# Attention's output stores moved from SyncE's queue to ScalarE's, in a one-core decoder step

## The chip, the cores and the metric

One Trainium2 chip, one core of it. The kernel is one launch. Its time is device microseconds of that core; the time before is the median of three runs, 2228.45 us (2225.63 to 2229.6). One more execution was profiled, and the rows below are from it.

Engines: PE is TensorE, DVE VectorE, ACT ScalarE, POOL GpSimd, SP SyncE. SP computes nothing here; it issues DMAs. A DMA that an engine issues stands in that engine's instruction stream: what it waits for, everything behind it on that engine waits for too.

## The reference

One step of a two-layer decoder trunk, float32, for a prompt of 1024 tokens and 8 samples of one token each: a pooling mixer and a gated ConvFFN, then keys and values (shared) and queries, dilated attention, and a second ConvFFN. The change lies in the prompt's attention. It has three groups of 8 heads of 64, with dilations 1, 4 and 16, in blocks of 128 queries that see their own block and the one before:

```
s = einsum('bnqrhe,bnkrhe->bnrhqk', qb, kk)
s = where(mask, s, NEG_INF)
lse = logsumexp(s, axis=-1)
p = exp(s - lse)
o = einsum('bnrhqk,bnkrhe->bnqrhe', p, vv)
...
wts = softmax(stack(lses))          # over the three groups
o = sum(wts * stack(outs))
```

## The kernel before

The work runs in stages, one behind the other on every engine: pooling, ConvFFN 0, projection of k, v and q (into DRAM, `kvs` and `qs`), attention, merge (the weighted sum of the groups, and the output projection w_o), ConvFFN 1. In attention, some 205 us long, every engine has one unrolled loop over half-steps.

**Steps.** `STEPS` (L2080) has 24 steps of 128 queries: 8 for dilation 1, 8 for dilation 4, 8 for dilation 16. Step s has two half-steps, i = 2s and 2s + 1, of four heads each (`NH` is 48). A step is wide if it also sees the block before: steps 1 to 7 and the odd ones of 9 to 15. The rest are narrow.

**One half-step i.** PE (`pe_attention`, L2234) makes the scores of i, turns (transposes) the queries or keys of the next step, turns the probabilities of i - 1 (`turn_p`) and multiplies those of i - 2 with v (`outputs`, L2297). DVE (`dve_attention`) takes the negated maxima of i (`maxima`, L2362) into `osb`, copies the turned queries or keys (L2354), copies the turned probabilities of i - 1 (L2366), and copies the outputs of i - 2 into `osb` (L2372, L2373; the second counts `at_oc`); in between it reduces one product of the samples' scores (L2390). ACT (`act_attention`, L2460) makes four exponentials of i (L2470), each with a row sum into `osb`, counted by `at_e`, and, for a wide i - 1, copies half of its turned probabilities (L2476). POOL multiplies the samples' cached keys (`kc`) with their queries (`qb`).

**osb and its stores.** `osb` has three slots, one a step (s % 3): outputs, maxima and sums, 528 floats for each of 128 queries. `store_o(e, s)` (L2222) waits for `at_oc` and `at_e` at 2s + 2 and issues the slot's store into `os_` in DRAM: one DMA of 264 KB for dilations 1 and 4, two of 132 KB for dilation 16. `maxima` of step s waits, from step 3 on, for the store of step s - 3 to have landed (L2360):

```
if s >= 3:
    v.wait_ge(rows_out[s % 3], ROWS + moved(s - 3, 3))
```

**SP's loop** (`sp_attention`, L2139) has 27 passes. Pass s issues, in this order: the queries of step s + 1 (`load_q`, waits for PE to have turned those of s - 1), k and v of step s (`load_kv`, into a ring `kvt` of four; waits for PE's outputs of step s - 3 if that is wide, else of s - 4), the store of step s - 3, two sample loads (`load_sample`; a buffer of `kc` waits for POOL's product), one of five copies to the outputs, cached values of one sample in passes 11 to 14 and 17 to 20 (`load_v`, L2210), and in pass 24 three quarters of w_o (`load_wo`, L2501). After it `sp_merge` (L2504) waits for all stores and loads `om` out of `os_`. ACT's merge begins with the splits of w_o (L2654).

Of the kernel before, what the change touches and what calls it, by code (L numbers as in the profile page):

```python
# [59 lines left out]
def build(nc, a, o):  # L60

    with ExitStack() as ctx:
# [2020 lines left out]
        NSTEP, NH = len(STEPS), 2 * len(STEPS)  # L2083

        def tile_rows(src, s):

            g, n, r, _ = STEPS[s]
            if g == 0:
                return [(slice(0, P), src[n * P:(n + 1) * P, :])]
            if g == 1:  # L2090
                return [(slice(0, P), src.rearrange("(m r) c -> r m c", r=4)[r, n * P:(n + 1) * P, :])]
            v = src.rearrange("(u r) c -> r u c", r=16)
            return [(slice(64 * e, 64 * e + 64), v[2 * n + e]) for e in range(2)]
# [9 lines left out]
        def wide(i):  # L2103

            return STEPS[i // 2][3]

        def span(i):

            return 2 * P if wide(i) else P
# [29 lines left out]
        def sp_attention(sp):  # L2139

            sp.wait_ge(pj_pe, 27 * GROUPS)

            def load_q(s):
                if s >= 2:
                    sp.wait_ge(at_tp, 2 * s - 3)
                for part, src in tile_rows(qs[STEPS[s][0], 0:T], s):
                    sp.dma_start(qt[part, s % 2, :], src).then_inc(at_q[s % 2], 16)

            def load_kv(s):
                if s >= 4:  # L2150
                    sp.wait_ge(at_o, 2 * s - 4 if STEPS[s - 3][3] else 2 * s - 6)
                for part, src in tile_rows(kvs[STEPS[s][0], 0:T].rearrange("t c n -> t (c n)"), s):
                    sp.dma_start(kvt[part, s % 4, :], src).then_inc(at_kv[s % 4], 16)

            def load_sample(n):
                s, g = n // 3, n % 3
                if g == 0:
                    if s >= 2:
                        sp.wait_ge(sm_p, n - 3)
                    sp.dma_start(qb[:, s % 2, :, :], qs[:, T + s, :].partition_broadcast(P)).then_inc(sm_q[s % 2], 16)  # L2160
                if n >= 3:
                    sp.wait_ge(sm_p, n - 2)
                sp.dma_start(kc[0:KEYS[g], n % 3, :], a[CACHES[g]][s, ::DIL[g], 0].rearrange(
                    "t h e -> t (h e)")).then_inc(sm_k[n % 3], 16)

            load_q(1)
            load_kv(1)
            sp.wait_ge(pj_h, 12 * GROUPS)
            sp.wait_ge(pj_l, 12 * GROUPS)
            for i in range(3):  # L2170
                sp.wait_ge(rows_out[i], ROWS)
            for g in range(GROUPS):
                sp.dma_start(qn[:, g, :], qs[g, T:N, :]).then_inc(in_new, 16)
                sp.dma_start(stage[0:NS, g, :], kvs[g, T:N].rearrange("t c n -> t (c n)")).then_inc(in_new, 16)
            sp.dma_start(samp[:, :], a["samp"]).then_inc(in_new, 16)
            for s in range(NSTEP + 3):
                if 1 <= s < NSTEP:
                    if s + 1 < NSTEP:
                        load_q(s + 1)
                    if s > 1:  # L2180
                        load_kv(s)
                if s >= 3:
                    store_o(sp, s - 3)
                for n in (2 * s - 4, 2 * s - 3):
                    if 0 <= n < ST:
                        load_sample(n)
                if 4 <= s < 4 + len(KV_PARTS):

                    g, first, rows, name = KV_PARTS[s - 4]
                    dst = (o[name + "_prompt"][0] if first < T else o[name + "_sample"][:, 0]).rearrange("t c h e -> t c (h e)")  # L2190
                    at = first - (T - WIN[g]) if first < T else 0
                    sp.dma_start(dst[at:at + rows], kvs[g, first:first + rows]).then_inc(out_w, 16)
                if s == 17:
                    sp.wait_ge(sm_p, ST)
                    sp.dma_start(diag, a["diag"]).then_inc(in_diag, 16)
                for n in {11: [4], 12: [5], 13: [6], 14: [7], 17: [0], 18: [1], 19: [2], 20: [3]}.get(s, []):
                    load_v(sp, n)
                if s == NSTEP:
                    sp.wait_ge(sm_st, 12)
                    for k in range(3):  # L2200
                        load_wo(sp, k)
# [8 lines left out]
        def load_v(e, s):  # L2210
            if s == 3:
                e.wait_ge(sm_o, 3)
            for g in range(GROUPS):
                e.dma_start(values_of(s, g)[0:KEYS[g], :], a[CACHES[g]][s, ::DIL[g], 1].rearrange(
                    "t h e -> t (h e)")).then_inc(sm_vin[s % 3], 16)
# [6 lines left out]
        def store_o(e, s):  # L2222
            e.wait_ge(at_oc, 2 * s + 2)
            e.wait_ge(at_e, 2 * s + 2)
            for part, dst in tile_rows(os_[STEPS[s][0]], s):
                e.dma_start(dst, osb[part, s % 3, :]).then_inc(rows_out[s % 3], 16)

        def scores_out(i):


            b = 2 * (i % 2)
            return ps[:, b:b + 2, 0:2 * span(i)].rearrange("p b (h n) -> p b h n", h=2)
# [227 lines left out]
        def act_attention(act):  # L2460
            for i in range(NH + 2):
                if i < NH:
                    s, n = i // 2, span(i)
                    act.wait_ge(at_m, i + 1)
                    if i >= 2:
                        act.wait_ge(at_pt, i - 1)
                    src = scores_out(i)
                    for j in range(4):
                        h = 4 * (i % 2) + j
                        ins = nc.scalar.activation(prob[:, i % 2, j * n:(j + 1) * n], src[:, j % 2, j // 2, :], ACT.Exp,  # L2470
                                                   bias=osb[:, s % 3, QW + h:QW + h + 1],
                                                   accum_out=osb[:, s % 3, QW + HEADS + h:QW + HEADS + h + 1])
                    ins.then_inc(at_e, 1)
                if 0 < i <= NH and wide(i - 1):
                    act.wait_ge(at_pt, i)
                    nc.scalar.activation(probT[:, (i - 1) % 2, 512:1024], ps[:, 5, :], ACT.Copy).then_inc(at_pb, 1)  # L2476
                if i == H_SM:
                    act.wait_ge(sm_st, 1)
                    nc.scalar.activation(sall, ps[0:64, 5, 0:SK], ACT.Exp, bias=stat[:, 0:1],
                                         accum_out=stat[:, 1:2]).then_inc(sm_e, 1)  # L2480

        def pool_attention(q):
            q.wait_ge(pj_r, 5 * 18 * GROUPS)
            q.wait_ge(pj_s, 1 + 7 * 18 * GROUPS)
            nc.gpsimd.memset(pT, 0.0).then_inc(sm_z, 1)
            for n in range(ST):
                s, g = n // 3, n % 3
                if g == 0:
                    q.wait_ge(sm_q[s % 2], 16 * (s // 2 + 1))
                q.wait_ge(sm_k[n % 3], 16 * (n // 3 + 1))  # L2490
                wait(q, sm_r, n)
                nc.gpsimd.tensor_tensor(prod[0:KEYS[g], 0, :], kc[0:KEYS[g], n % 3, :], qb[0:KEYS[g], s % 2, g, :],
                                        ALU.mult).then_inc(sm_p, 1)
# [7 lines left out]
        def load_wo(e, k):  # L2501
            e.dma_start(stage[:, k % 3, :], a["w_o"][0, k * P:(k + 1) * P, :]).then_inc(piece_in[k % 3], 16)
# [251 lines left out]
        @block.sync  # L2754
        def _(sp):
            sp_start(sp)

            def begin0(e, n):
                if n == 1:
                    sp_pool_tails(e)  # L2760
                    e.wait_ge(wp_l, 1)
                    e.wait_ge(wp_h, 1)
            sp_ffn(sp, 0, ffn[0], begin0, pool_x)
            sp_project(sp)
            sp_attention(sp)
            sp_merge(sp)

            def begin1(e, n):
                e.wait_ge(wo_h, 4)
                e.wait_ge(wo_l, 4)  # L2770
            sp_ffn(sp, 1, ffn[1], begin1, wo_x)

            sp.wait_ge(out_w, 16 * (3 + len(KV_PARTS)))
            sp.wait_ge(tl_out, 32)
            sp.wait_ge(ct_out[0], 32 * 6 * DEPTH)
            sp.wait_ge(ct_out[1], 32 * 5 * DEPTH)
            sp.wait_ge(y_out, 16 * STORES)
# [132 lines left out]
```

## Time and profile before

| | |
|---|---|
| median of three runs | 2228.45 us |
| the profiled execution | 2229.66 us |
| its span in the trace | 2227.8 us |
| attention in it | about 1225 to 1430 us |
| busy: PE, DVE, ACT, POOL | 97%, 69%, 44%, 22% |
| mean DMA rate | 172 GB/s |
| queue q1 (issued by SP) | 284.24 MB, 39.5% of 16 engines |
| queue q10 (issued by ACT) | 4.68 MB, 0.6% |

The 1.9 us between span and time lie around the program. All times of rows are microseconds from the start of the span, unless ns is written. A group of instructions has its line in the kernel, its engine, its operation, output<-input by the program's names, and xcount. Brackets at the end of a timeline's row tell how long the engine was idle before it, and what released it. DMA-issuing instructions (SPq, ACTq) take part in the engine's order but are not counted as busy; the time to landing is from the issue until the data is there.

### The profile page before, as it was taken

The page shows a single profiled execution, that of the slowest core. Times are in us where ns is not written, and L with a number is a line of the kernel's source. Part 1 is how long each engine was busy: PE and PEld are TensorE (multiplying, and loading weights), DVE is VectorE, ACT ScalarE, POOL GpSimd, SP SyncE. Part 2 cuts the span into 40 slices and gives each one's busy share as a digit, 9 for nine tenths or more (in the row PEclk, how much of TensorE's full clock was granted, in tenths as well). Part 3 has the DMA queues.
Part 4 walks back from the last instruction along what each step waited for, and adds up shares of the span by engine and source line. Part 5 has one row for each costly group of instructions (what it writes and reads, how often), then busy time and mean ns, then how long its engine had stood idle before and what let it go on. Part 6 is the DMA issues. An engine that isn't in the chain of part 4 may idle for free.

```text
span 2227.8 us, 43164 instructions
## 1 busy us (share of the span) xinstructions
PE 2171.4 (97%) x16008; PEld 2022.9 (91%) x16019; DVE 1536.4 (69%) x2375; ACT 988.5 (44%) x1868; POOL 480.2 (22%) x674
## 2 busy tenths in 40 slices
PE   7999999999999999999999999999999999999998
PEld 7999999999999977777777887598999999999998
DVE  4778888887656677365463777676888888875554
ACT  4655555555434533122121444455555555554342
POOL 1002223222200145053251220010122233221000
PEclk8999999999999999999999999999999999999999
DMA  6225777788985522222232797631467777889764
GB/s 188 86 83 162 200 207 189 190 216 214 295 258 180 171 94 81 100 81 95 95 104 103 244 285 195 188 124 48 129 171 206 208 192 200 205 228 318 213 193 140
DMA packets 243995, 383.28 MB, mean 172 GB/s; under 512 B 21736, under 2 KB 117784, under 8 KB 241971
## 3 DMA queue, kind: packets, MB, share of 16 engines
q1 hardware_dynamic: 207778, 284.24, 39.5%
q0 software_dynamic: 31328, 92.66, 19.1%
q10 hardware_dynamic: 4760, 4.68, 0.6%
q8 instruction: 80, 1.31, 0.2%
q14 instruction: 49, 0.39, 0.1%
HBM read 303.65 MB, written 173.98 MB: 214 GB/s over the span
## 4 chain that ended last, share of the span: by engine, by line
PE 91%; DVE 4%; DMA 3%; ACT 2%; issue 1%; SPq 0%; ACTq 0%; POOL 0%; DVEq 0%; POOLq 0%
PE ps L1233 38%; PE ps L1323 20%; PE ps L2065 6%; PE ps L2067 6%; PE ps L2066 6%; PE ps L2297 2%; PE ps L2710 2%; PE ps L2270 1%; DMA kvt<-kvs 1%; PE ps L2281 1%; PE ps L418 1%; PE ps L2237 1%; PE ps L853 1%; PE ps L2059 1%; PE ps L2060 1%; PE ps L479 1%
## 5 line engine op out<-in xcount | busy, mean ns | idle before, releaser
L1233 PE MATMUL ps<-hT,w 128*128 128x258 f32 x2752 | 462.1, 285 | 4.2 <-DVE w L1075 2.3
L1233 PEld LDWEIGHTS ps<-hT,w 128*128 128x128 f32 x2752 | 388.1, 191 | 5.1 <-DVE w L1075 2.7
L1233 PE MATMUL ps<-lT,w 128*128 128x258 f32 x1376 | 278.2, 284 | 0.0
L1233 PE MATMUL ps<-hB,w 128*128 128x258 f32 x1344 | 231.7, 284 | 3.7 <-DVE ub L1434 3.7
L2065 PE MATMUL ps<-wq,xh 128*128 128x512 f32 x576 | 227.7, 395 | 0.9 <-DVE wq L1892 0.9
L2067 PE MATMUL ps<-wq,xl 128*128 128x512 f32 x576 | 227.4, 395 | 0.0
L2066 PE MATMUL ps<-wq,xh 128*128 128x512 f32 x576 | 226.9, 394 | 0.0
L1233 PEld LDWEIGHTS ps<-lT,w 128*128 128x128 f32 x1376 | 215.2, 191 | 0.0
L1323 PE MATMUL ps<-gdh,wda 128*128 128x258 f32 x1184 | 198.9, 284 | 0.0
L1233 PEld LDWEIGHTS ps<-hB,w 128*128 128x128 f32 x1344 | 193.1, 192 | 4.1 <-DVE ub L1434 4.1
L1323 PE MATMUL ps<-gdh,wdb 128*128 128x258 f32 x1152 | 193.4, 284 | 0.0
L1323 PEld LDWEIGHTS ps<-gdh,wda 128*128 128x128 f32 x1184 | 166.7, 190 | 0.7 <-DVE gdl L1523 0.3
L1323 PEld LDWEIGHTS ps<-gdh,wdb 128*128 128x128 f32 x1152 | 161.7, 189 | 0.7
L1233 PE MATMUL ps<-lB,w 128*128 128x258 f32 x672 | 136.7, 285 | 0.0
L1184 ACT ACTIVATE w<-sq 128x1024 fp32r<-128x1024 f32 x84 | 89.0, 1059 | 107.6 <-PE ps L1233 91.9
L2065 PEld LDWEIGHTS ps<-wq,xh 128*128 128x128 f32 x576 | 108.2, 188 | 29.9 <-DVE wq L1892 4.3
L1459 DVE SCALAR_TENSOR_TENSOR ca<-ua,cwT,ca 128x1024 f32<-128x1024 f32 x88 | 112.8, 1281 | 28.8 <-ACT ca L1689 28.2
L1557 POOL DMA_DIRECT2D wsum<-in_w_down x44 | 24.1, 554 | 501.7 <-DMA stage<-in_w_up 423.4
L2067 PEld LDWEIGHTS ps<-wq,xl 128*128 128x128 f32 x576 | 108.0, 188 | 25.4
L2066 PEld LDWEIGHTS ps<-wq,xh 128*128 128x128 f32 x576 | 108.2, 188 | 25.1
L1560 POOL DMA_DIRECT2D wsum<-in_w_down x88 | 80.3, 1096 | 225.6 <-DMA stage<-in_w_up 176.0
L2470 ACT ACTIVATE prob<-ps,osb 128x128 f32<-128x128 f32 (+1 forms) x192 | 77.2, 414 | 106.3 <-DVE osb L2362 106.3
(338 smaller groups left out, 4839.2 us busy)
## 6 DMA issues: line engine op xcount, KB each, us to landing
stage<-in_w_up SPq DMA_DIRECT2D x176, 256.0 KB, 3.8
wsum<-in_w_down POOLq DMA_DIRECT2D x132, 256.0 KB, 5.4
gs<-cb SPq DMA_DIRECT2D x44, 516.0 KB, 6.7
stage<-wsum SPq DMA_DIRECT2D x88, 256.0 KB, 3.0
tsum<-gs POOLq DMA_DIRECT2D x66, 258.0 KB, 7.4
tsum<-gneg POOLq DMA_DIRECT2D x66, 258.0 KB, 7.9
stage<-in_w_down SPq DMA_DIRECT2D x58, 256.0 KB, 3.1
stage<-in_w_kv SPq DMA_DIRECT2D x24, 512.0 KB, 3.9
```

The lines of the kernel that those rows point to most:

```text
L1184: nc.scalar.activation(out, src, ACT.Copy).then_inc(f_hi, 1)
L1233: mm = pe.matmul(ps[:, bank + c, 0:HB], w, m[:, c * HB:(c + 1) * HB], start=(first and i == 0), stop=(i == len(parts) - 1), skip_group_che ...
L1323: mm = pe.matmul(ps[:, 2 * d + c, 0:HB], w, m[:, c * HB:(c + 1) * HB], start=(i in FRESH and p == 0 and j == 0), stop=(last and j == 2), s ...
L1459: nc.vector.scalar_tensor_tensor(out=c[:, 0:T], in0=u[:, t:t + T], scalar=w, in1=c[:, 0:T], op0=ALU.mult, op1=ALU.add).then_inc(f_conv, 1)
L1557: q.dma_start(dst, src).then_inc(sums_in, 16)
L1560: q.dma_start(dst, src, accum_op=ALU.add, max_dma_last_dim=4 * N).then_inc(sums_in, 16)
L2065: pe.matmul(out, xh[:, k, tok], W, start=(k == 0), stop=False)
L2066: pe.matmul(out, xh[:, k, tok], Wt, start=False, stop=False)
L2067: mm = pe.matmul(out, xl[:, k, tok], W, start=False, stop=(k == KC - 1))
L2297: mm = pe.matmul(ps[:, 6, j * P:(j + 1) * P], probT[:, i % 2, n * P:(n + 1) * P], v, start=(w == 0), stop=(w == len(tiles) - 1))
L2470: ins = nc.scalar.activation(prob[:, i % 2, j * n:(j + 1) * n], src[:, j % 2, j // 2, :], ACT.Exp, bias=osb[:, s % 3, QW + h:QW + h + 1], ...
L2710: mm = pe.matmul(ps[:, bank0 + n, 0:NW], w, m[:, c * NW:(c + 1) * NW], start=(i == 0), stop=(i == len(parts) - 1))
```

## The change

SP issues no store of `osb` any more. ACT issues that of step i / 2 - 2 in its half-step i, for even i from 4 on, behind the exponentials of i and the copy of i - 1, and the last one after its loop. Waits, sizes, order of the stores and semaphores are the same.

```diff
@@ sp_attention, SP's loop
                         load_q(s + 1)
                     if s > 1:
                         load_kv(s)
-                if s >= 3:
-                    store_o(sp, s - 3)
                 for n in (2 * s - 4, 2 * s - 3):
                     if 0 <= n < ST:
                         load_sample(n)
@@ act_attention, ACT's loop
                 if 0 < i <= NH and wide(i - 1):
                     act.wait_ge(at_pt, i)
                     nc.scalar.activation(probT[:, (i - 1) % 2, 512:1024], ps[:, 5, :], ACT.Copy).then_inc(at_pb, 1)
+                if i >= 4 and i % 2 == 0:
+                    store_o(act, i // 2 - 2)
                 if i == H_SM:
                     act.wait_ge(sm_st, 1)
                     nc.scalar.activation(sall, ps[0:64, 5, 0:SK], ACT.Exp, bias=stat[:, 0:1],
                                          accum_out=stat[:, 1:2]).then_inc(sm_e, 1)
+
+            store_o(act, NSTEP - 1)
```

## Rows read from the trace of the kernel before

**Rows 1.** The page: the chain that ended last, shares of the span by engine
```profile
PE 91%; DVE 4%; DMA 3%; ACT 2%; issue 1%; SPq 0%; ACTq 0%; POOL 0%; DVEq 0%; POOLq 0%
```

**Rows 2.** Stretches: length, busy time of each engine, PE clock, DMA share, GB/s
```profile
1297.00:1345.00 48.00, 43.81 (x417) 38.29 (x419) 36.52 (x70) 21.76 (x96) 15.07 (x12) 1.00 0.94 289
...
1405.00:1430.00 25.00, 23.54 (x212) 20.28 (x211) 19.75 (x45) 13.61 (x66) 0.00 (x0) 1.00 0.57 160
```

**Rows 3.** Waits of PE, 1225 to 1440: us in total, times, longest
```profile
PE ps L2237 <- DMA kvt<-kvs: 4.9, 5, 1.9
```

**Rows 4.** Timeline of PE: start, duration, instruction, idle before; keys of steps 12, 13
```profile
1328.26 0.66 PE L2237 MATMUL ps<-ident,kvt 128*128 128x128 f32 x4 [1.87 <-DMA kvt<-kvs]
...
1336.60 0.66 PE L2237 MATMUL ps<-ident,kvt 128*128 128x128 f32 x4 [0.94 <-DMA kvt<-kvs]
```

**Rows 5.** Waits of SP's queue, 1220 to 1500: us in total, times, longest
```profile
SPq L2226 <- DVE osb L2373: 45.4, 14, 5.0
```

**Rows 6.** Timeline of SP's issues, passes 11 to 13
```profile
1309.84 0.43 SPq L2153 DMA_DIRECT2D kvt<-kvs  x1
1314.19 0.33 SPq L2226 DMA_DIRECT2D os_<-osb  x1
...
1316.44 2.39 SPq L2214 DMA_DIRECT2D vlate<-in_cache_kv_w  x3
...
1321.45 0.33 SPq L2153 DMA_DIRECT2D kvt<-kvs  x1
...
1326.67 0.43 SPq L2153 DMA_DIRECT2D kvt<-kvs  x1
```

**Rows 7.** Tiles osb and y: stores issued, ns min/median/max; landing of osb's, us
```profile
L2226 SPq DMA_DIRECT2D os_<-osb x32: 326/448/1246, 1240.5 to 1430.5; - x32
...
DMA to landing us min/median/max: 2.0/4.0/7.0
...
L1798 ACTq DMA_DIRECT2D out_y_prompt<-yst x10: 379/483/1915, 2121.0 to 2224.1; - x10
```

**Rows 8.** Timelines of DVE and ACT around the maxima of step 12
```profile
1324.16 0.69 DVE L2390 TENSOR_REDUCE sq<-prod 128x8 f32<-128x512 f32 x1 [2.21 <-POOL prod L2492]
...
1327.38 0.48 ACT L2470 ACTIVATE prob<-ps,osb 128x256 f32<-128x256 f32 x1
...
1331.71 0.67 DVE L2362 TENSOR_REDUCE osb<-ps 128x4 f32<-128x512 f32 x1
```

**Rows 9.** Timelines, steps 20 and 21: ACT, SP, DVE, ACT, PE
```profile
1406.62 0.37 ACT L2470 ACTIVATE prob<-ps,osb 128x128 f32<-128x128 f32 x1
...
1410.06 1.11 SPq L2226 DMA_DIRECT2D os_<-osb  x2
...
1410.41 0.69 DVE L2362 TENSOR_REDUCE osb<-ps 128x4 f32<-128x512 f32 x1 [0.38 <-PE ps L2270]
...
1411.13 0.37 ACT L2470 ACTIVATE prob<-ps,osb 128x128 f32<-128x128 f32 x1 [1.16 <-DVE osb L2362]
...
1413.56 0.60 PE L2281 MATMUL ps<-ident,prob 128*128 128x128 f32 x4
```

**Rows 10.** DMA issues: KB each, median us to landing; 1300 to 1345, then 1405 to 1425
```profile
os_<-osb SPq DMA_DIRECT2D x5, 264.0 KB, 6.1
...
stage<-in_w_o SPq DMA_DIRECT2D x3, 512.0 KB, 6.5
...
os_<-osb SPq DMA_DIRECT2D x6, 132.0 KB, 2.3
```

**Rows 11.** Timelines of SP, ACT and DVE at attention's end
```profile
1411.21 1.24 SPq L2153 DMA_DIRECT2D kvt<-kvs  x2
...
1422.30 1.55 SPq L2502 DMA_DIRECT2D stage<-in_w_o  x3
...
1430.69 1.06 ACT L2654 ACTIVATE woh<-stage 128x1024 fp32r<-128x1024 f32 x1 [0.18 <-DMA stage<-in_w_o]
...
1437.20 0.18 DVE L2529 TENSOR_REDUCE ow<-om 128x8 f32<-128x24 f32 x1 [3.77 <-DMA om<-os_]
```

## The prediction

> **What bounds the kernel now.** I read the chain that ended last first [rows 1]: TensorE (PE) carries 91% of it, DMA 3%, ScalarE (ACT) 2%. A change on the queues of ACT and SP pays only where PE stands still for them. Then the stretches of attention [rows 2]: in the middle one, 1297 to 1345 us, PE is idle for 4.2 us of 48 and the DMA engines are 94% busy; in the last, 1405 to 1430, PE is idle for 1.5 us of 25 and the DMA engines are 57% busy. Next, whom PE waits for between 1225 and 1440 us [rows 3]: 4.9 us in five waits for loads of kvt, and any help for the loads must come out of them. The timeline of PE shows the waits singly; the two that matter here are 1.87 and 0.94 us [rows 4], for the k of steps 12 and 13.
>
> What do the stores do to SP? Its own waits [rows 5] name 45.4 us in 14 waits at L2226 for DVE's last copy of a step. That looks large, but most of what stands behind the wait could not start anyway. load_q(s+2), the next in line after the samples, needs the queries of step s turned, which PE does one half-step after the outputs that store_o(s-3) waits for. After a wide step load_kv(s), ahead of the store, waits for the same outputs (at_o 2s-4) itself. So the store holds back only the sample loads, the cache values (load_v) and the output copies, and those only where step s-3 is narrow and load_kv(s) needs two half-steps less.
>
> [Rows 6] show such a place: kvt of step 11 is issued at 1309.84, the store at 1314.19 as soon as DVE lets it, and load_v at 1316.44 behind the store and the samples; then kvt of step 12 at 1321.45, when PE has freed its buffer, and that of step 13 only at 1326.67, behind a store, three sample loads (one waits for POOL's product), three of load_v and the queries: 9 issues in 5.2 us, 4.5 at 0.5 each, and 0.7 of waiting.
>
> **Removed from SP.** 24 calls of store_o, 32 DMAs (16 of 264 KB, 16 of 132 KB), 32 x 0.448 = 14.3 us of issuing [rows 7], and the 45.4 us of waiting. What it is worth:
> - *Step 12's load.* The samples and load_v between 1314.5 and 1318.8 can go after 1310.3, so some 1.5 to 4 us earlier, bounded by POOL's products, for which kc's buffers wait. The load that PE misses is issued by PE's own outputs, so only its landing can improve, with 1.5 us less of backlog before it: 1.4 of the 1.87 us.
> - *Step 13's load.* One store issue (0.4) and the 0.7 of waiting go, if the samples come earlier, so it is issued about 1.1 us earlier; against a wait of 0.94 us, but PE also asks for it 1.4 us earlier by the first point. I take 0.4.
> - *The other three waits* (4.9 - 1.87 - 0.94 = 2.1) are for loads that PE's outputs release: nothing. Their bounds are 0 and all 2.1 us.
> - *DVE's 2.21 us wait for POOL's product* [rows 8] goes with the earlier samples; it lies beside PE's wait for kvt, so it is worth 0 by itself.
> Sum: -1.8 us, bounds 0 and -4.9 (all of the waits for kvt).
>
> **Added to ACT.** 32 issues. The nearest rows are the same store on SP, 0.33 to 1.25 us, median 0.45, and ACT's own stores of y, median 0.48 [rows 7]. The wait is no wait: store_o(i/2-2) wants at_oc and at_e at i-2; DVE makes the copies of half-step i-3 before maxima(i), and ACT has already waited for maxima(i). Issuing stands behind the exponentials of an even half-step, in ACT's idle time before the next: 1.16 us before those of 1411.13 in narrow steps [rows 9], for two DMAs that took SP 1.11 us, and more in wide ones. If it overran, PE would ask for these probabilities at 1413.56, when four exponentials of 0.37 us from 1411.13 are over at 1412.6: 0.95 us in reserve. Zero, cover named; without it some 0.5 us a step.
>
> **Moved: the store leaves later.** This is the real cost. Before, it left when DVE had copied the outputs, in half-step 2s-3; now, behind the exponentials of half-step 2s-2. DVE's maxima(2s) waits for it to have landed (L2360), and behind that wait stand DVE's copies of qT and probT, and behind those ACT and PE.
> - *Middle stretch.* The store for step 12 now leaves after the exponential that begins at 1327.38 and takes 0.48; the maxima come at 1331.71 [rows 8]: 3.8 us. PE turns these probabilities behind the k of step 13, which began at 1336.60 [rows 4], some 0.5 later; without its wait of 0.94 that is 1336.1, and maxima (0.68) and exponentials (1.5) are over at 1333.9: 2.2 us in reserve. So a landing up to 6.0 us is free. The median for a 264 KB store there is 6.1 us [rows 10], over all stores 4.0 and at most 7.0 [rows 7]. It happens at the four even steps 10 to 16. I take 0.1 us each, 0.4; bounds 0 and 4 x 1.4 = 5.6 (7.0 + 0.45 of issue - 6.0).
> - *Last stretch.* From the end of the exponentials of step 20 (1406.62 + 0.37) to the maxima of step 21 at 1410.41 are 3.4 us, with the 0.95 in reserve 4.35 [rows 9]. A pair of 132 KB stores takes 0.55 for the first issue and 2.3 from the second to landing [rows 10]: 2.9, free. But w_o moves too: load_wo stood behind store_o(21) at 1422.30; with no stores it follows kvt of step 23, at 1411.21 before and about 1410 now [rows 11]. So 1.5 MB of weights land beside the stores of steps 19 and 20, which steps 22 and 23 wait for. I take the landing as the mean of 2.3 and w_o's own 6.5 [rows 10], 4.4, since the two share the DMA engines and neither row is nearer: (0.55 + 4.4 - 4.35) x 2 = 1.2 us. Bounds 0 and 5.4 (2 x 2.7).
> - *Tail.* The last store waits for the same copy on either engine. It stands ahead of ACT's three splits of w_o (1.06 each), which end near 1434 instead of 1431.8; DVE's are then done before the first om lands at 1437.20 [rows 11]. Zero. That w_o is there early is also worth nothing.
>
> At 1309.84 to 1316.44 SP stood waiting while loads were due [rows 6], so I count earlier starts as gain. The Trainium skill (DMA: Bandwidth & Descriptors, "Issuing engines are not separate DMA queues") has it that a second issuing engine saves only the sequencer's time of initiating, not transfer time. By that rule step 12's load would gain nothing: the first rival below.
>
> **Sum.** -1.8 + 0.4 + 1.2 = -0.2 us. The profiled execution took 2229.66 us for a span of 2227.8, 1.2 above the median of 2228.45; I put the change on the median: 2228.2. A difference below 0.2%, 4.5 us, is about what a measurement of this kernel can't tell from no change.
>
> **Rivals.**
> - *Hidden anyway* (0.22): SP's idle time was never the bound, the loads land as before, and so do the stores: 2228.4. It is what the skill's page just named would have. For it: 94% DMA share where PE waits, and three of five waits are released by PE itself.
> - *The loads are really freed* (0.09): all five waits vanish and stores land in time: 2228.45 - 4.9 = 2223.5. Against it: a buffer of kvt still comes free only with PE's outputs.
> - *A new wait on DVE for osb* (0.14), the other side: stores land over 6.0 us in the middle stretch or over 4.35 in the last. Price with w_o's 6.5 us in the last stretch 5.4, and up to 5.6 in the middle; with a third of the latter and the gain of 1.8 kept, +5.5: 2233.9, up to 2237.7. It decides from the landing times just named. For it: the median landing sits on the limit in the middle. Against it: part of those 6.1 us is waiting behind loads in SP's own queue, which the store no longer does.
> - *Stores cut into the loads* (0.10): a store used to stand behind kvt in one queue, and now runs beside it from another. 264 KB (0.27 MB) at 289 GB/s [rows 2] are 0.9 us for each of the five late loads: +4.6, with the gain of 1.8 kept +2.8: 2231.2. The Trainium skill (DMA: Bandwidth & Descriptors, Queues, rings and completion order) says that each DMA engine takes turns between queues by packet, which is this case; no row of before has two such queues at work in attention.
> The change can hardly fail to do what it says: the calls are unrolled, and no condition hangs on data.
>
> **Numbers.** The forecast with its small terms has 0.45. Faster by over 0.2%: the freed loads and a little of the forecast, 0.10. Slower by over 0.2%: most of DVE's new wait and a bit of the last rival, 0.14. The rest 0.76. The range of 8 in 10 leaves out the far halves of the second and third rivals: 2224.0 to 2232.8.
>
> **What would show it.** All 32 issues of os_ stand on ACTq with about 0.45 us each, and SP has no wait for DVE's copy. Step 12's wait for kvt falls to about 0.5 us, and load_v comes near 1312. w_o is issued near 1411. DVE's maxima at L2362 name DMA os_ as releaser for under 2 us in sum: over 5 us there, and PE idle for kT, qT or prob in 1405 to 1430, would be the third rival; unchanged waits for kvt and none new, the first. The forecast is wrong if PE's idle time between 1225 and 1430 changes by over 4 us in sum.

## The result, and the profile after

| | before | after |
|---|---|---|
| median | 2228.45 us (9 runs, 2225.49 to 2232.18) | 2241.81 us (9 runs, 2231.91 to 2245.04) |
| ratio, 95% interval | 1 | 1.0046 [1.0034, 1.0059] |
| span of the execution profiled | 2227.8 us | 2230.1 us |

The kernel is slower by some 10 us, where it was forecast to be faster by 0.2, with an upper end of 2232.8. A second set of runs on another chip (`e8_after_again`) gave 1.0045 [1.0032, 1.0058]. The medians here differ by 13.4 us, the ratios say 10; I take 10 us, 0.45% of 2230. The profile shown with this result is of the fastest of its runs; the second profile below is nearer to the median.

The span of that fastest run is only 2.3 us longer than before's. That number misleads. Attention, from VectorE's first maxima to its last copy of outputs, is 7.0 us longer; the part ahead of attention, where the two kernels are the same, happened to be 3.6 us shorter. The stretch of attention, first in before, then in after, then in the second profile of after (length; busy time of PE, PEld, DVE, ACT, POOL; PE clock; DMA share; GB/s):

```profile
1228.90:1429.80 200.90, 190.31 (x1698) 158.01 (x1710) 147.62 (x284) 94.28 (x410) 30.43 (x24) 1.00 0.76 226
```

```profile
1225.30:1433.20 207.90, 195.02 (x1709) 160.95 (x1710) 146.86 (x284) 93.08 (x408) 30.47 (x24) 0.98 0.71 218
```

```profile
1227.80:1437.00 209.20, 192.70 (x1698) 159.09 (x1710) 146.79 (x284) 92.90 (x408) 30.43 (x24) 0.99 0.72 217
```

PE's idle time in it is 10.6, 12.9 and 16.5 us. The rest of the difference is PE being busy longer at a lower mean clock. How far to trust one profile is taken up at e2_ring4 below.

In the page of after, the chain that ended last by line now names stores among its larger shares, where before did not, and 6.5 MB went from q1, SP's queue, to q10, ACT's.

```profile
q1 hardware_dynamic: 204194, 277.74, 38.1%
...
q10 hardware_dynamic: 8344, 11.17, 1.5%
...
PE ps L1233 39%; PE ps L1323 20%; PE ps L2065 6%; PE ps L2067 6%; PE ps L2066 6%; PE ps L2712 2%; PE ps L2295 2%; DMA os_<-osb 1%; PE ps L2268 1%; PE ps L418 1%; PE ps L2279 1%; PE ps L853 1%; PE ps L2235 1%; PE ps L2059 1%; PE ps L2060 1%; PE ps L479 1%
```

The tile view of osb in after: the stores now stand on ACTq, and the maxima wait for them. (Lines have moved: maxima L2362 is now L2360, the store L2224; L2153 and L2163 are as before.)

```profile
L2224 ACTq DMA_DIRECT2D os_<-osb x32: 325/414/684, 1239.4 to 1434.0; - x32
...
  DMA os_<-osb: 14.4, 8
...
DMA to landing us min/median/max: 2.2/4.2/10.9
```

Against [rows 7]: issuing is as cheap as it was on SP. The longest landing went from 7.0 to 10.9 us, and VectorE waits 14.4 us in 8 waits where it had none. The median over all stores hardly moved (4.0 to 4.2), but it mixes stretches. Taken by stretch, the median went from 5.3 to 9.7 us in 1262 to 1300, from 6.1 to 7.1 in 1300 to 1345, from 2.3 to 4.2 in 1405 to 1425; in between it is about the same. Where the waits are, from the timelines of ACT, DVE and PE, with the longest and the two in the last stretch:

```profile
1296.85 0.37 ACT L2468 ACTIVATE prob<-ps,osb 128x128 f32<-128x128 f32 x1 [1.96 <-DVE osb L2360]
1296.93 0.33 ACTq L2224 DMA_DIRECT2D os_<-osb  x1
...
1307.95 1.23 DVE L2360 TENSOR_REDUCE osb<-ps 128x4 f32<-128x1024 f32 x1 [4.21 <-DMA os_<-osb]
1309.92 0.63 PE L2235 MATMUL ps<-ident,kvt 128*128 128x128 f32 x4 [2.32 <-DVE qT L2352]
...
1414.16 0.69 DVE L2360 TENSOR_REDUCE osb<-ps 128x4 f32<-128x512 f32 x1 [0.70 <-DMA os_<-osb]
...
1420.19 0.69 DVE L2360 TENSOR_REDUCE osb<-ps 128x4 f32<-128x512 f32 x1 [1.18 <-DMA os_<-osb]
```

The store of step 6, issued at 1296.93, landed just before 1307.95, so the maxima of step 9 waited 4.21 us, DVE's copy of the next queries with them, and PE stood 2.32 us for that copy. The other five waits are two in the wide stretch (0.92 at 1267.01, step 5, and 2.55 at 1278.19, step 6) and three at steps 10, 12 and 14 (0.71, 2.19 and 1.95). The last two shown are of steps 21 and 22.

Why 10.9 us? What the queues moved from the issue of step 6's store on, 1296.9 to 1301 and then 1301 to 1308:

```profile
q1 hardware_dynamic: 392, 0.86, 56.4%
```

```profile
q1 hardware_dynamic: 816, 2.21, 82.9%
q10 hardware_dynamic: 144, 0.27, 10.6%
```

For the first 4 us q1 moved 0.86 MB and q10 nothing: the store's own packets had not begun. Then both moved side by side until it was done. So the landing is long in two parts, a late first packet and shared engines after it. A store that met an empty q1 (e5_wo_late, issued at 1418.47) had packets moving about a microsecond later and was done soon after 1421.

What SP does with its freedom, against [rows 6] and [rows 11] (timeline of SP in after, and PE's waits for the keys of steps 12 and 13, which answer to [rows 4]):

```profile
1313.18 1.45 SPq L2212 DMA_DIRECT2D vlate<-in_cache_kv_w  x3
...
1326.75 0.66 PE L2235 MATMUL ps<-ident,kvt 128*128 128x128 f32 x4 [0.17 <-DMA kvt<-kvs]
1336.46 1.12 PE L2235 MATMUL ps<-ident,kvt 128*128 128x128 f32 x4 [2.29 <-DMA kvt<-kvs]
...
1414.11 2.79 SPq L2504 DMA_DIRECT2D stage<-in_w_o  x3
```

load_v went 3.3 us earlier, as forecast, and PE's wait for step 12 fell from 1.87 to 0.17. The gain was given back at once: step 13's grew from 0.94 to 2.29. w_o is issued at 1414.11, right behind the last load of kvt and 8 us earlier than before.

### The profile page after: what moved, and what is told of

Its sections match the earlier page's. It is cut to its first block, busy times and chain, and to the rows that moved or that the text cites. A ratio compares the mean times of both kernels' runs of the same rounds, so it can differ in the third digit from the quotient of the medians.

```text
span 2230.1 us, 43175 instructions
## 1 busy us (share of the span) xinstructions
PE 2173.0 (97%) x16019; PEld 2022.7 (91%) x16019; DVE 1535.3 (69%) x2375; ACT 989.0 (44%) x1868; POOL 480.7 (22%) x674
## 3 DMA queue, kind: packets, MB, share of 16 engines
q0 software_dynamic: 31328, 92.66, 19.1%
## 4 chain that ended last, share of the span: by engine, by line
PE 90%; DVE 4%; DMA 3%; ACT 2%; issue 1%; SPq 0%; ACTq 0%; POOL 0%; DVEq 0%; POOLq 0%
PE ps L1233 39%; PE ps L1323 20%; PE ps L2065 6%; PE ps L2067 6%; PE ps L2066 6%; PE ps L2712 2%; PE ps L2295 2%; DMA os_<-osb 1%; PE ps L2268 1%; PE ps L418 1%; PE ps L2279 1%; PE ps L853 1%; PE ps L2235 1%; PE ps L2059 1%; PE ps L2060 1%; PE ps L479 1%
```

## The experiments

The kernel before ran on the same chip beside each group of versions: medians 2229.84 (e1 to e4), 2230.16 (e5, e7 to e9) and 2230.67 us (e10 to e12). Clock means are over all runs of a kernel; before has 0.9848, 0.9852 and 0.9850.

| run | change to | median us | ratio to before [95%] | mean clock |
|---|---|---|---|---|
| e8_after_again | none, after | 2239.70 | 1.0045 [1.0032, 1.0058] | 0.9840 |
| e5_wo_late | after | 2233.54 | 1.0015 [1.0006, 1.0024] | 0.9855 |
| e2_ring4 | after | 2230.22 | 1.0002 [0.9991, 1.0013] | 0.9852 |
| e1_odd | after | 2234.82 | 1.0023 [1.0013, 1.0033] | 0.9838 |
| e9_odd_spwait | after | 2233.13 | 1.0011 [1.0002, 1.0019] | 0.9845 |
| e7_odd_ring4 | after | 2230.62 | 1.0002 [0.9992, 1.0012] | 0.9850 |
| e10_ring4_wolate | after | 2232.96 | 1.0007 [0.9995, 1.0018] | 0.9847 |
| e11_odd_ring4_wolate | after | 2232.10 | 1.0010 [0.9995, 1.0024] | 0.9844 |
| e3_late_sp | before | 2240.99 | 1.0044 [1.0031, 1.0057] | 0.9832 |
| e4_dve_fill | before | 2236.07 | 1.0030 [1.0020, 1.0041] | 0.9837 |
| e12_wo_early_sp | before | 2231.74 | 1.0007 [0.9995, 1.0020] | 0.9843 |

**Four slots of osb (e2_ring4).** This takes away what the wait is for.

```diff
-        osb = sb("osb", [P, 3, OW], F32, r1)
+        osb = sb("osb", [P, 4, OW], F32, r1)
...
-                if s >= 3:
-                    v.wait_ge(rows_out[s % 3], ROWS + moved(s - 3, 3))
+                if s >= 4:
+                    v.wait_ge(os_out[s % 4], (ROWS if s % 4 < 3 else 0) + moved(s - 4, 4))
```

> The changed kernel with four slots of osb in place of three; the maxima of step s wait for the store of step s-4. Both 'late' and 'queue': the waits for os_ vanish and the time is 2225 to 2230 us, with a mean clock of 0.986. Rival 'loads' (the cost is what the stores and the early w_o do to the loads of kvt): the time stays above 2235.

Measured 2230.22, 1.0002 of before: the whole loss is gone within what can be told (the interval is 2.5 us to either side), with the stores still on ACT, still late, and w_o still early. Its stores land as slowly as in after, so it is not the landing that hurts but that someone needs it. Tile view of osb in e2_ring4; the line "DMA os_<-osb" under the idle times of its engines is not there any more:

```profile
L2226 ACTq DMA_DIRECT2D os_<-osb x32: 326/414/1392, 1241.8 to 1436.7; - x32
...
DMA to landing us min/median/max: 2.2/4.8/10.7
```

The rival 'loads' falls: the time is not above 2235. PE's waits for kvt are longer in its profile, 7.3 us against 4.9, but that costs nothing that the medians see.

This run is also a warning about single profiles. Its attention is 208.3 us long, as long as after's, in a kernel that is no slower than before; the profiled run was 4.7 us above the median, and PE's mean clock in attention was 0.97, where before's one profile has 1.00. A stage of one profile shows where waits are; what they cost is taken from the medians.

**On time on ScalarE (e1_odd).**

```diff
-                if i >= 4 and i % 2 == 0:
-                    store_o(act, i // 2 - 2)
+                if i >= 3 and i % 2 == 1:
+                    store_o(act, (i - 3) // 2)
...
-            store_o(act, NSTEP - 1)
```

> The changed kernel, but ScalarE issues the store of step (i-3)/2 in odd half-steps i, so about when SyncE did before. Theory 'late': the store leaves a half-step too late for the maxima that need its slot; then VectorE's waits for os_ fall from 14.4 us to under 2 and the time to 2225 to 2230 us. Rival 'queue': a store in ScalarE's own queue lands late beside SyncE's loads whenever it is issued (10.9 us once); then waits of over 5 us stay, and the time stays at 2233 to 2242.

Measured 2234.82, 1.0023. By the ratios half of the loss (1.0046 to 1.0023) goes with the half-step. Its profile, of its fastest run (2228.79), shows no wait for os_ at all, but landings of up to 9.0 us. Neither theory is right alone: 5 us stay, and in this profile they can't be seen. The mean clock is 0.9838 in place of 0.9848, by the sum under e4_dve_fill some 2.4 us of these 5, with nearly as much spread. Two kernels on this footing narrow it down.

**The same with a fourth slot (e7_odd_ring4)**, both diffs above.

> Stores on ScalarE in odd half-steps and four slots of osb. Theory 'queue' for what was left of the odd kernel's cost (5 us): a store in its own queue sometimes lands too late even when issued on time; then the fourth slot takes it away, 2227 to 2231 us. Rival 'freed SyncE' (sample loads and cached values go earlier and get into the way of the loads of kvt): 2233 to 2236 as without the slot.

Measured 2230.62, 1.0002. The rest of the cost goes with the need for a landing, not with the freed SP, though e1's profile shows no such wait.

**The same, SP as slow as before (e9_odd_spwait).**

```diff
+                if s >= 3:
+                    sp.wait_ge(at_oc, 2 * s - 4)
                 for n in (2 * s - 4, 2 * s - 3):
                     if 0 <= n < ST:
                         load_sample(n)
```

> Stores on ScalarE in odd half-steps, three slots, and SyncE keeps the wait for the outputs' copy that it had in front of each store, without the store: what it issues goes when it did before. 'Freed SyncE': the odd kernel's remaining cost goes, 2228 to 2231 us. 'Queue': it stays, 2233 to 2236.

Measured 2233.13, 1.0011 [1.0002, 1.0019]. The time lies at the lower edge of the range for 'queue'; against e1 it is 1.7 us less, on another chip and with overlapping intervals, so it is no verdict by itself. This wait also puts w_o back to its old place (1421.83). With e7 it fits a store that sometimes comes too late from its own queue, and a part of that through w_o; neither part is shown.

**Late on SyncE (e3_late_sp).**

```diff
                 if s >= 3:
+                    if 2 * s - 1 <= NH:
+                        sp.wait_ge(at_m, 2 * s - 1)
                     store_o(sp, s - 3)
```

> The kernel before, stores still on SyncE, but each waits also for the maxima of half-step 2s-2, which is when ScalarE issues them in the changed kernel. 'Late': VectorE waits for os_ 8 to 16 us in sum and the time is 2234 to 2243 us. 'Queue': in SyncE's queue they land as before; waits under 3 us, 2228 to 2231.

The time fits 'late' (2240.99), but for another reason, and I had not foreseen it: the wait on SP also held everything behind it. Waits of PE in e3_late_sp, 1225 to 1445 us, and the landing of its stores:

```profile
PE ps L2239 <- DMA kvt<-kvs: 12.1, 7, 4.1
...
DMA to landing us min/median/max: 2.0/2.6/7.4
```

VectorE never waits for os_ here, while PE waits 12.1 us for kvt instead of 4.9 [rows 3]. So it does not show that lateness alone makes the wait. It shows two other things: a store that leaves late, with the loads held behind it, lands in 2.6 us in the median, where ACT's queue has 4.2 (after), 4.6 (e8) and 4.8 (e2), which fits time spent beside SP's loads; and holding SP's loads back costs as much as the whole change did.

**A second profile of after (e8_after_again).**

> The changed kernel once more, for a second profile: the first was its fastest run (2231.9 us where the median is 2241.8). If the stores' landing is the cause throughout, a profile near 2240 us shows VectorE waiting for os_ more than the 14.4 us of the first, 18 to 30 us, and a clock of 0.984 or less. If the typical loss were elsewhere, the waits for os_ stay near 14 and another row grows.

The profile's run took 2238.91 us. VectorE waits 19.1 us in 9 waits, 5 us more than in the first profile, as expected; 4.62 of it is one wait in the last stretch. Timelines of SP, ACT, DVE and PE there:

```profile
1413.59 1.53 SPq L2504 DMA_DIRECT2D stage<-in_w_o  x3
...
1414.62 0.45 ACTq L2224 DMA_DIRECT2D os_<-osb  x1
1415.11 0.62 ACTq L2224 DMA_DIRECT2D os_<-osb  x1
...
1423.11 0.69 DVE L2360 TENSOR_REDUCE osb<-ps 128x4 f32<-128x512 f32 x1 [4.62 <-DMA os_<-osb]
...
1424.55 1.09 PE L2235 MATMUL ps<-ident,kvt 128*128 128x128 f32 x4 [2.93 <-DVE qT L2352]
```

Three DMAs of w_o go out, the store of step 19 goes a microsecond later on the other queue, and it is there only at 1423.1: 8.0 us after its second issue. The queues show the same two parts as before. From 1414.6 to 1418 q1 moves 0.89 MB and q10 nothing; the whole store moves between 1418 and 1423, beside the rest of w_o:

```profile
q1 hardware_dynamic: 259, 0.89, 96.0%
```

```profile
q1 hardware_dynamic: 289, 1.03, 57.7%
q10 hardware_dynamic: 160, 0.27, 14.6%
```

In the first profile of after the same pair took 4.7 us from its second issue and the wait was 1.18. Only step 22 waits for a store that meets w_o: step 23 waits in neither profile, and the wait of step 21 (0.70, and 0.88 here) ended as w_o was being issued and is in e5 too (0.83).

And then TensorE's clock. Stretches of 10 us, PE busy, granted clock, DMA share, GB/s; first of e8_after_again, then of before:

```profile
1420.00:1430.00 10.00, 7.07 (x56) 0.83 0.29 93
...
1450.00:1460.00 10.00, 9.09 (x49) 0.66 0.49 157
1460.00:1470.00 10.00, 9.59 (x51) 0.66 0.32 109
```

```profile
1420.00:1430.00 10.00, 8.54 (x72) 1.00 0.65 212
...
1450.00:1460.00 10.00, 10.00 (x54) 0.66 0.33 106
1460.00:1470.00 10.00, 8.61 (x65) 1.00 0.76 237
```

In before, the stretch from 1420 has full clock (2.4 GHz); here, after PE stood 2.93 us, the mean is 0.83, a third of those 10 us at the lower level (1.2 GHz). Part of the merge is slow in before too (0.66 from 1450); here a further 10 us are at 0.66. That part can't be put down to this wait: from 1430 to 1480 the mean is 0.86 here and 0.86 in e5, which has no such wait, against 0.93 in before and in the first profile of after.

**w_o at its old place (e5_wo_late).**

```diff
                 if s == NSTEP:
                     sp.wait_ge(sm_st, 12)
+                    sp.wait_ge(at_oc, 44)
```

> The changed kernel, but SyncE waits for the outputs of step 21 before it issues w_o, so that w_o goes when it did before. Theory: w_o beside the stores of steps 19 and 20 costs 1 to 3 us through VectorE's waits at half-steps 42 and 44; then 2238 to 2241 us. If it costs nothing: 2241 to 2243.

Measured 2233.54, 1.0015, beside 2239.70 on the same chip: 6.2 us by the medians, twice the highest figure expected. It is the largest single part. Its profile has w_o at 1422.92 and no wait for os_ after 1412.56; 13 us of such waits stay before 1351, and what is left of the loss is 3.4 us by the medians. So the sum of the waits is no measure of their cost: 13 us of them go with 3.4 us here, while what e5 gives back, 6.2 us, stands in the profiles as one wait of 1.18 or 4.62.

**w_o early without the second queue (e12_wo_early_sp)**: in before, the three loads of w_o are put in pass 23 ahead of store_o(20).

```diff
                 if s >= 3:
+                    if s == NSTEP - 1:
+                        sp.wait_ge(sm_st, 12)
+                        for k in range(3):
+                            load_wo(sp, k)
                     store_o(sp, s - 3)
...
-                if s == NSTEP:
-                    sp.wait_ge(sm_st, 12)
-                    for k in range(3):
-                        load_wo(sp, k)
```

> The kernel before, stores on SyncE, but w_o issued in pass 23 ahead of the store of step 20. Theory: what hurts in the changed kernel's last stretch is 1.5 MB of weights in front of or beside a store that VectorE waits for, whichever queue; here VectorE waits for os_ 1 to 4 us at half-step 46 and the time is 2231 to 2235 us. If it needs the second queue: no wait, 2229 to 2231.

Measured 2231.74, 1.0007 [0.9995, 1.0020]: not told from before, and a wait a little under the 1 to 4 us expected. The mechanism is there, small, in the timelines of SP and DVE:

```profile
1415.32 1.53 SPq L2502 DMA_DIRECT2D stage<-in_w_o  x3
1418.44 15.54 SPq L2226 DMA_DIRECT2D os_<-osb  x8
...
1424.81 0.69 DVE L2362 TENSOR_REDUCE osb<-ps 128x4 f32<-128x512 f32 x1 [0.83 <-DMA os_<-osb]
```

One store is behind w_o here, and it had more time (issued at 1418.44, needed near 1424); PE's waits for probabilities behind these 0.83 us are 0.44 and 0.34, where before has one of 0.79. That w_o hurts in the changed kernel because the stores it meets are late already fits this and is not shown apart.

**The stall without any DMA (e4_dve_fill)**: before, with 24 reductions into a scratch tile on VectorE. They are extra work and leave the outputs as they are.

```diff
+                for n in range(*{10: (0, 2), 12: (2, 6), 18: (6, 13), 20: (13, 14), 24: (14, 18), 28: (18, 21), 42: (21, 22), 44: (22, 24)}.get(i, (0, 0))):
+                    nc.vector.tensor_reduce(fill[:, 8 * n:8 * n + 8], kT[:, (s - 1) % 3, :].rearrange('p (h e) -> p h e', h=HEADS),
+                                            AX.X, ALU.add)
```

> The kernel before, with 24 reductions of 0.6 us (14.4 us) added on VectorE ahead of the maxima of half-steps 10, 12, 18, 20, 24, 28, 42 and 44, where the changed kernel's profile shows its waits for os_ of that size; no DMA is touched. Theory 'clock' (TensorE's starved stretches cost a drop of its clock on top): 2235 to 2243 us, with mean clocks of 0.981 to 0.984 in several runs. Rival: only the stall itself counts, +2 to +5 us, 2230 to 2233.5, clock 0.985 or more.

Measured 2236.07, 1.0030. The reductions took 0.676 us each, 16.2 us in all and not the 14.4 that were planned. They cost 6.7 us with no DMA touched. The mean clock is 0.9837 in place of 0.9848: 0.0011 x 2230 = 2.5 us of full clock lost. So by this estimate somewhat over a third of the cost is the clock and the rest the stall; the spread of the single runs leaves some 2 us to either side of the 2.5. For the change itself the same sum from e8 gives 0.0012 x 2230 = 2.7 us of its 10. In e5 the mean clock is not lower than before's (0.9855), so what is left of the loss there does not come from it.

In the profile of e4 there is a drop in the stretch with the largest delay (columns as in [rows 2]; before had 1.00 there):

```profile
1297.00:1345.00 48.00, 41.73 (x350) 36.53 (x348) 38.19 (x72) 19.22 (x85) 12.69 (x10) 0.89 0.82 257
```

That drop is no proof that the delays brought it. The same stretch has 0.93 in e2, e7 and e11, which have no wait for os_ and are not told from before. They have waits of PE for kvt there, 3.0 to 3.4 us the longest. And a wait does not always bring a drop: near 1358 PE stood 2.99 us for kT in before and the next 4 us had 1.00; in after it stood 2.76 and they had 0.70.

The Trainium skill (TensorE: Matmul & The Clock Gate, Part 1) describes this as a gate: the throttled state is the default and activity releases it. These rows agree in direction only: the drops in attention stand behind waits of PE, but not every wait is followed by one.

**Everything undone but the queue (e10 and e11).** e10 is e2 with w_o late, e11 is e7 with w_o late.

> The changed kernel with four slots of osb and w_o issued only after step 21's outputs. If VectorE's wait for the landing of stores is all that the change costs, w_o's place is worth nothing once the fourth slot is there: 2229 to 2231 us, as with the slot alone (2230.2). If w_o early costs something besides that wait: 2226 to 2228.

> Stores in odd half-steps on ScalarE, four slots, w_o late: every suspected cost of the change undone, only the freed SyncE left. If freeing SyncE brings the 1.8 us that were forecast: 2227 to 2229 us against 2230 of before. If it brings nothing: 2229.5 to 2231.

Measured 2232.96 and 2232.10, with 1 inside both intervals. Both lie 1 to 2 us above every range expected, so neither expectation was met to the letter; beside a before of 2230.67 they read as no gain. The lower ends of the intervals, 0.9995, leave room for 1.1 us, not for the 1.8 forecast. Freeing SP brings nothing that can be seen even with each cost removed: PE's waits for kvt are 5.2 us in three waits in e11's profile, against 4.9 in five. That the two are nominally 2 us above e2 and e7, which have w_o early, is less than these comparisons can tell; no worth of w_o's place is seen once the slot is there. No version beat the kernel before.

## Why the prediction was wrong

**The third rival was what happened**, with its place and the point from which it decides: DVE's maxima waiting for osb, in the last stretch beside w_o and in the middle one. The forecast that was put first was wrong, the range too narrow, and the chance of 0.14 too small. Its price of +5.5, up to 9.2, was also below the 10 measured.

**The step that failed: "Moved: the store leaves later", by the size of both its terms.**
- *Last stretch, 1.2 us, bound 5.4.* w_o's move was foreseen, with its place. Its price was not: w_o late gives 6.2 us back (e5). I took the landing as 4.4 us and bounded it with w_o's own 6.5, for two waits; there was one, and its landing was 8.0 in e8 (4.7 in the first profile). In e8 the store issued behind 1.5 MB on the other queue had no packet moving until 3.4 us after its first issue, and it was done at about the same time as w_o. My argument against the rival, that ACT's queue spares the store the wait behind SP's loads, did not hold.
- *Middle stretch, 0.4 us, bound 5.6.* What is left with w_o late is 3.4 us. I counted the four even steps 10 to 16. Three of them did wait, but the longest wait was at step 9, which follows a narrow step, and two were in the wide stretch, which I had left out. I took the largest landing seen on SP's queue, 7.0, as the bound; it was 10.9.
- *What no term had.* A wait was priced as the wait less the reserve. The mean clock also fell, by the estimate 2.5 of e4's 6.7 us and 2.7 of the change's 10; that the waits brought it down is the likely reading, not shown apart.

**The sign that was named for a wrong forecast did not come.** PE's idle time between 1225 and 1430 was to change by over 4 us. It is 12.1 us in before, 12.2 in the first profile of after and 15.8 in the second. A fixed window of the trace is the wrong measure: attention had begun earlier and ended later than the window, and time lost to a lower clock counts as busy.

**The gain of 1.8 us.** The forecast for step 12 was right in its row (1.87 to 0.17; 0.5 was expected) and wrong in the sum: the next load took it back. e7, e10 and e11, where costs are undone, show no gain; "hidden anyway" was right about SP. The rule of the Trainium skill that was weighed there (DMA: Bandwidth & Descriptors, "Issuing engines are not separate DMA queues"), that a second issuing engine saves sequencer time only, agrees with these three.

**Stores cut into the loads** did not show in the time. PE's waits for kvt are longer where the stores are on ACT's queue with a fourth slot, 5.2 to 7.3 us in e2, e7, e10 and e11 against 4.9, but the medians are not told from before.

**What was right:** issuing costs nothing that is seen (0.414 us each; e2 and e7 keep all 32 issues on ACT), nor does the tail, w_o is issued early, and the place of the new wait in the last stretch.

**What stays open:** how e1's remaining 5 us divide between w_o and late landings elsewhere; e9 removed w_o's part and the median fell by 1.7 us, inside the noise between two chips. Whether lateness alone, on one queue with nothing held behind it, would make the wait; e3 did not test that cleanly. And why a store's first packet comes 3 to 4 us late beside a filled other queue.

## What to carry to other kernels

A store that frees a buffer has a deadline like a load. Before moving one, write down for every reuse the time from the new issue to the wait, and compare it with the longest landing that could occur beside everything the move lets go earlier on the other queue, not with a median. If the slack is thin, one more slot of the buffer (2 KB a partition here) is the cheap remedy. Look at landings stretch by stretch, and price a stall from several runs: its clock may go with it, and the length of one profiled run may hide it.

## What the runs showed that was not expected

- In these traces ACT's DMA goes out at the start of the exponentials it stands behind: 1296.93 for the store, 1296.85 for the first of the four, before any has ended. The store was therefore less late than reckoned, by about 1.4 us, and still too late.
- Which queue a store is on hardly changed its median landing over the whole stage, 4.0 to 4.2 us, and nearly doubled it in the wide stretch, 5.3 to 9.7 (9.9 in e8).
- A store on the second queue did not share the DMA engines from its issue on. For 3.4 us (e8) and 4 us (step 6) only the other queue's packets moved.
- The nine runs of after range over 13 us where before's nine range over 7. That alone shows nothing: before's 29 runs beside e10 range over 12, and e7, which costs nothing, over 13. What told the versions apart was the median of several runs, not one run and not one profile.
